# Memory keys and values of a two-block decoder kernel: the norm's root moves into the operand, values are made with tokens on rows, ScalarE copies them, and their blocks are dealt out over seven places

## What is computed

```python
def second_block(x, mem, mem_norm_gain, ...):
    mem_n = rms_norm_2(mem, mem_norm_gain)
    for layer in range(DEPTH):            # DEPTH = 2
        y = mlstm_mixer(...) if layer == 0 else stick_breaking_mixer(...)
        x = x + rms_norm_2(y, g[1])
        y = memory_cross_attention(rms_norm_2(x, g[2]), mem_n, xa_w_q, xa_w_kv, xa_w_o)
        x = x + rms_norm_2(y, g[3])
        y = swiglu_ffn(rms_norm_2(x, g[4]), ffn_w_gate_up, ffn_w_down)
        x = x + rms_norm_2(y, g[5])

def memory_cross_attention(h, mem_n, w_q, w_kv, w_o):      # XA_HEADS = 4, XA_HEAD_DIM = 256
    q = (h @ w_q).reshape(B, S, XA_HEADS, XA_HEAD_DIM)
    kv = (mem_n @ w_kv).reshape(B, 256, 2, XA_HEADS, XA_HEAD_DIM)
    k, v = kv[:, :, 0], kv[:, :, 1]
    s = einsum('bthd,bmhd->bhtm', q, k) * (XA_HEAD_DIM ** -0.5)
    o = einsum('bhtm,bmhd->bthd', softmax(s), v).reshape(B, S, D_MODEL)
    return o @ w_o
```

## Time and profile before

| | us |
|---|---|
| median of 3 runs (1766.02 to 1771.69) | 1766.06 |
| the profiled execution | 1770.89 |
| its span | 1769.1 |
| TensorE busy in it | 1690.5 (96%) |
| VectorE busy | 1186.5 (67%) |
| ScalarE busy | 936.5 (53%) |
| GpSimd busy | 332.4 (19%) |

### The profile page before, as it was taken

The page is one execution under the profiler, slowest core; times in us unless marked ns, Lnnn a source line. Parts: engine busy times, 40 slices in busy tenths (PEclk is TensorE's granted clock), DMA queues, the critical chain, the costliest instruction groups (busy, mean ns, idle before and its releaser), DMA issues.

```text
span 1769.1 us, 32699 instructions
## 1 busy us (share of the span) xinstructions
PE 1690.5 (96%) x13204; PEld 1615.9 (91%) x13204; DVE 1186.5 (67%) x2027; ACT 936.5 (53%) x1659; POOL 332.4 (19%) x304
## 2 busy tenths in 40 slices
PE   6999999999999989999999999999989999989997
PEld 6898889999997889999888999999979998889997
DVE  6999887555577745556577665866666667476665
ACT  5677765544455646544555444544455644454443
POOL 0100011243412112345111100000252110000025
PEclk8999999999999999999999999999999999989999
DMA  5433334555532245555334534455644343335663
GB/s 179 132 120 108 120 108 143 166 171 177 179 93 80 81 140 184 187 187 185 129 118 146 167 120 155 155 170 184 181 147 136 127 156 118 107 118 172 185 184 106
DMA packets 76325, 257.47 MB, mean 146 GB/s; under 512 B 8464, under 2 KB 12560, under 8 KB 75920
## 3 DMA queue, kind: packets, MB, share of 16 engines
q1 hardware_dynamic: 76176, 255.39, 45.1%
HBM read 254.31 MB, written 1.05 MB: 144 GB/s over the span
## 4 chain that ended last, share of the span: by engine, by line
PE 77%; DVE 12%; ACT 6%; issue 4%; POOL 1%; DMA 0%; POOLq 0%; DVEq 0%; SPq 0%; ACTq 0%
PE pb L140 75%; DVE WL L159 2%; DVE TMP L171 2%; DVE SCR L171 2%; ACT SCR L149 1%; ACT L156 1%; DVE SCR L159 1%; PE pb L143 1%; ACT WH L149 1%; DVE HNL L171 1%; POOL SCR L159 1%; ACT TMP L149 1%; ACT ASH L149 1%; DVE ASL L171 0%; ACT Rbuf L149 0%
## 5 line engine op out<-in xcount | busy, mean ns | idle before, releaser
L140 PE MATMUL pb<-HNH,WH 128*128 128x256 f32 (+1 forms) x2120 | 613.9, 290 | 6.1 <-DVE WL L159 1.9
L159 DVE TENSOR_TENSOR WL<-RAW,WH 128x1024 fp32r<-128x1024 f32 (+4 forms) x514 | 604.9, 1177 | 10.4 <-ACT WH L149 10.0
L140 PE MATMUL pb<-HNH,WL 128*128 128x256 f32 (+1 forms) x2120 | 603.1, 284 | 0.0
L140 PE MATMUL pb<-HNL,WH 128*128 128x256 f32 (+1 forms) x2120 | 602.8, 284 | 0.0
L149 ACT ACTIVATE WH<-RAW 128x1024 fp32r<-128x1024 f32 (+4 forms) x514 | 507.2, 989 | 154.7 <-PE pb L140 147.1
L140 PE MATMUL pb<-ASH,WH 128*128 128x256 f32 (+1 forms) x1688 | 493.4, 292 | 11.1 <-DVE WL L159 7.1
L140 PE MATMUL pb<-ASH,WL 128*128 128x256 f32 (+1 forms) x1688 | 483.2, 286 | 0.0
L140 PE MATMUL pb<-ASL,WH 128*128 128x256 f32 (+1 forms) x1688 | 482.9, 286 | 0.0
L140 PEld LDWEIGHTS pb<-HNH,WH 128*128 128x128 f32 x2120 | 402.1, 190 | 14.3 <-issue 6.8
L140 PEld LDWEIGHTS pb<-HNH,WL 128*128 128x128 f32 x2120 | 402.4, 190 | 0.0
L140 PEld LDWEIGHTS pb<-HNL,WH 128*128 128x128 f32 x2120 | 400.6, 189 | 1.0
(11 more groups left out here) (149 smaller groups left out, 1454.3 us busy)
## 6 DMA issues: line engine op xcount, KB each, us to landing
RAW<-in_w_gu SPq DMA_DIRECT2D x88, 512.0 KB, 3.8
RAW<-in_w_up SPq DMA_DIRECT2D x64, 512.0 KB, 3.5
RAW<-in_w_down SPq DMA_DIRECT2D x64, 512.0 KB, 3.5
RAW<-in_w_ssd SPq DMA_DIRECT2D x48, 512.0 KB, 3.5
RAW<-in_w_xkv SPq DMA_DIRECT2D x32, 512.0 KB, 3.5
RAW<-in_w_mlin SPq DMA_DIRECT2D x24, 512.0 KB, 3.5
RAW<-in_w_fd SPq DMA_DIRECT2D x32, 384.0 KB, 3.0
RAW<-in_w_sbqkv SPq DMA_DIRECT2D x24, 512.0 KB, 4.1
```

The costliest lines, as they stand in the source:

```text
L140: return self.eng.matmul(o, l, r, start=start, stop=stop, skip_group_check=skip) if self.eng else Nothing()
L159: return self.eng.tensor_tensor(o, a, b, op) if self.eng else Nothing()
```

## The change

- The memory chunks are multiplied by gain and root in place, once, by VectorE in steps 8 to 15 of `mlin` (`dve_mem_root`); the high and low parts are made from that without a scale. `RM` is not used when blocks leave PSUM any more.
- Values are made with tokens on the partitions: the memory's high and low chunks (128 tokens each) are the loaded operand, and the split weights are streamed, 256 columns (one head) at a time. A head's values take two blocks of weights as a pair, in two banks; both banks have to be free before the pair starts, and both are filled when it ends. The weights are laid out for this on the host.
- ScalarE copies keys and values out of PSUM (`act_fill`), where it waits for TensorE's end of the block or pair. VectorE only splits weights there. The transposes and the copies after them are gone.
- The fills are dealt out anew (in blocks): 5 in the last steps of mLSTM, 7 in the norm after `mlo`, 4 in the last steps of cross-attention 0, 5 in the norm after `xo0`, 5 in the norm after `fd0`, 2 in the last steps of the stick-breaking attention, 4 in the norm after `sbo`. In a norm one fill or none stands ahead of every second step m, and one fill (of two blocks) instead of two stands ahead of `pe_rest` after `sbo`.
- For the fills after `fd0` the memory's parts are made a third time (`mem2`), in `ASH[:, 0:8]`, during the eight last blocks of `fd0`.
- Cross-attention waits for the keys' copies at its first scores and for a head's value copies at that head's output product.

```diff
-    p += xkv[0][0:7] + out("mlo", xkv[0][7:16])
-    p += [("xq0", 0, m) for m in range(8)] + xkv[1][0:2] + out("xo0", xkv[1][2:8])
-    p += ffn(0)
-    p += [("sbqkv", 0, m) for m in range(24)] + xkv[1][8:12] + out("sbo", xkv[1][12:16])
+    p += xkv[0][0:5] + out("mlo", xkv[0][5:12])
+    p += [("xq0", 0, m) for m in range(8)] + xkv[0][12:16] + out("xo0", xkv[1][0:5])
+    p += ffn(0) + xkv[1][5:10]
+    p += [("sbqkv", 0, m) for m in range(24)] + xkv[1][10:12] + out("sbo", xkv[1][12:16])
...
-                q.wait_ge(*(eva if PLAN[i - 3][0] in ("up0", "up1", "wk") else evd)[i - 3])
+                q.wait_ge(*(eva if PLAN[i - 3][0] in ("up0", "up1", "wk", "xkv0", "xkv1") else evd)[i - 3])
...
-        FILL = {"mlo": [(0, "k", 7)] + [(0, "v", c) for c in range(8)],
-                "xo0": [(1, "k", m) for m in range(2, 8)], "sbo": [(1, "v", c) for c in range(4, 8)],
-                "xo1": [], "fd0": [], "fd1": []}
+        FILL = {"mlo": [("k", 0, 5), ("k", 0, 6), ("k", 0, 7), ("v", 0, 0), ("v", 0, 1)],
+                "xo0": [("k", 1, m) for m in range(5)],
+                "fd0": [("k", 1, 5), ("k", 1, 6), ("k", 1, 7), ("v", 1, 0)],
+                "sbo": [("v", 1, 2), ("v", 1, 3)], "xo1": [], "fd1": []}
+        FIRSTS = {"mlo": 2, "xo0": 2, "fd0": 2, "sbo": 1, "xo1": 0, "fd1": 0}
+
+        def fills_at(post, m):
+
+            rest = FILL[post][FIRSTS[post]:]
+            return rest[m // 2:m // 2 + 1] if m % 2 == 0 else []
...
+        def mem_parts(l, kind, m):
+            if l == 0:
+                return as_chunks("mem0", 8, 8, T2)
+            if kind == "k" and m < 5:
+                return as_chunks("mem0", 8, 8, T2)
+            if kind == "k" or m == 0:
+                return as_chunks("mem2", 0, 8, T2)
+            return as_chunks("mem1", 8, 8, T2)
+
+        def v_blocks(q, l, h):
+            return [q.block(f"xkv{l}", 0, 8 + 2 * h + j) for j in range(2)]
+
+        def pe_fill(q, kind, l, m):
+            xs = mem_parts(l, kind, m)
             if kind == "k":
+                pe_block(q, f"xkv{l}", 0, m, T2, xs)
+                return
+            ids = v_blocks(q, l, m)
+            for i in ids:
+                pe_bank_free(q, i)
+            for j in range(2):
+                q.wait_ge(*lo[ids[j]])
+                for t in range(2):
+                    o = bank_of(ids[t])[:, 0:256]
+                    for k in range(4):
+                        xh, xl, ready = xs[4 * j + k]
+                        wh = WH[:, ids[j] % NWS, 256 * k:256 * k + 256]
+                        wl = WL[:, ids[j] % NWS, 256 * k:256 * k + 256]
+                        q.wait_ge(*ready)
+                        q.matmul(o, xh[:, 128 * t:128 * t + 128], wh, j == 0 and k == 0, False)
+                        q.matmul(o, xl[:, 128 * t:128 * t + 128], wh, False, False)
+                        mm = q.matmul(o, xh[:, 128 * t:128 * t + 128], wl, False, j == 1 and k == 3)
+                mm.then_inc(*use(ids[j]))
+
+        def act_fill(q, kind, l, m):
+            if kind == "k":
+                i, b = act_block(q, f"xkv{l}", 0, m, T2)
+                q.wait_ge(*use[i])
                 if l:
                     q.wait_ge(*xs_[0, 3])
+                q.activation(KM[:, m, :], b, ACT.Copy).then_inc(*eva(i))
+                return
+            ids = v_blocks(q, l, m)
+            act_split(q, ids[1])
+            q.wait_ge(*use[ids[1]])
+            if l:
+                q.wait_ge(*xov[0, m])
+            for t in range(2):
+                q.activation(VM[:, t, 256 * m:256 * m + 256], bank_of(ids[t])[:, 0:256], ACT.Copy).then_inc(*eva(ids[t]))
+
+        def dve_fill(q, kind, l, m):
+            if kind == "k":
+                dve_block(q, f"xkv{l}", 0, m, T2)
             else:
+                dve_split(q, v_blocks(q, l, m)[1])
...
-            for f in fill[:2]:
+            for f in fill[:FIRSTS[post]]:
...
-                if m + 2 < len(fill):
-                    pe_fill(q, *fill[m + 2])
+                for f in fills_at(post, m):
+                    pe_fill(q, *f)
...
-        def act_mem(q, l, c):
-            q.wait_ge(s_mem, 16)
-            act_part(q, mem_tag(l), c, ASH[:, 8 + c, 0:T2], MR[:, c, :],
-                     use[AT["down1", 3, 7] if l == 0 else AT["fd0_5", 1, 7]], scale=cc("memn", c, 1))
-
-        def dve_mem(q, l, c):
-            q.wait_ge(*ah[mem_tag(l), c])
-            q.stt(ASL[:, 8 + c, 0:T2], MR[:, c, :], cc("memn", c, 1), ASH[:, 8 + c, 0:T2].bitcast(F32), ALU.mult,
-                  ALU.subtract).then_inc(*al(mem_tag(l), c))
+        def dve_mem_root(q, c):
+            q.wait_ge(*rms["mem"])
+            q.stt(MR[:, c, :], MR[:, c, :], cc("memn", c, 1), RM[:, :], ALU.mult, ALU.mult).then_inc(*memsc(c))
+
+        MEMPARTS = {"mem0": (8, lambda: use[AT["down1", 3, 7]]), "mem1": (8, lambda: use[AT["fd0_5", 1, 7]]),
+                    "mem2": (0, lambda: use[AT["fd0_5", 0, 7]])}
+
+        def act_mem(q, tag, c):
+            c0, free = MEMPARTS[tag]
+            act_part(q, tag, c, ASH[:, c0 + c, 0:T2], MR[:, c, :], free(), memsc[c])
+
+        def dve_mem(q, tag, c):
+            c0 = MEMPARTS[tag][0]
+            dve_part(q, tag, c, ASL[:, c0 + c, 0:T2], MR[:, c, :], ASH[:, c0 + c, 0:T2])
...
+        ML_FILL = [0, 1, 2, 4, 5]
...
-            return [(1, "k", n - 9)] if l == 0 and n > 8 else []
+            return [("v", 0, n - 6)] if l == 0 and n in (8, 9) else []
...
-                    q.wait_ge(*evd[AT[f"xkv{l}", 0, 7]])
-                    q.wait_ge(*xvc[l, 7])
+                    q.wait_ge(*eva[AT[f"xkv{l}", 0, 7]])
...
+                q.wait_ge(*eva[AT[f"xkv{l}", 0, 9 + 2 * h]])
...
                         act_block(q, fd_name(l, q4), q4 % 2, m, T2)
+                        if l == 0 and q4 == 3:
+                            act_mem(q, "mem2", m)
                         if q4 == 3:
                             act_square(q, post, m, Y[:, m, :], T2, yadd[l, 3, m])
...
                         i, b = dve_block(q, fd_name(l, q4), q4 % 2, m, T2)
+                        if l == 0 and q4 == 3:
+                            dve_mem(q, "mem2", m)
                         q.wait_ge(*use[i])
...
-                pe_fill(q, 1, "v", n - 24)
+                if n == 24:
+                    pe_fill(q, "v", 1, 1)
...
-        arr[f"xkv{l}"] = lay(f["xa_w_kv_2"][l], 1, 8)
+        kv = f["xa_w_kv_2"][l]
+        vv = kv[:, 1024:2048].reshape(2, 4, 128, 4, 256).transpose(3, 0, 2, 1, 4).reshape(1, 8, 128, 1024)
+        arr[f"xkv{l}"] = np.concatenate([lay(kv[:, 0:1024], 1, 8), vv], 1)
```

## The result

| | before | after |
|---|---|---|
| median of 10 runs each (before 1765.07 to 1773.45, after 1773.53 to 1781.91) | 1767.66 | 1777.43 |
| ratio, 95% interval | | 1.0046, 1.0030 to 1.0062 |
| profiled execution, its span | 1770.89, 1769.1 | 1781.91, 1780.1 |

The change makes the kernel slower by 0.46% in the ratio (8.1 us; the means are 1768.8 and 1776.9); the medians differ by 9.8 us, and the spans of the two profiled executions by 11.0. The forecast was 1776.

A forecast was written before the change was run, and what follows sets the result against it. TensorE, busy 96% of the span, was taken as the bound, so time could come only from its waits and small work. The terms summed to +9.7 us on a median of 1766.06, about 1776; range 1762 to 1787.

The forecast's parts named there:

- Point 3: Last eight `fd0` blocks: making `mem2` closes a ring of waits through four engines, 3.55 us a turn; +9.5 us.
- Rival A: The `mem2` loop in `fd0` doesn't bite, as TensorE has slack; about 1766 us, chance 0.15.
- Point 2: Norm after `fd0`: five fills, 14.3 us of blocks, lengthen it by only 7.5 us; -6.8 us.
- Point 1: Value blocks: 16 pairs of transposes go, most on a full TensorE; -3.4 us.
- Point 4: `sb` tail: two blocks instead of four leave waits of 3.4, 0.6 and 1.2 us; +5.0 us.
- Point 5: `ml` tail: two blocks fewer cost 5.7 us, an earlier root gives back 1.9; +3.8 us.
- Point 6: `mlo`, cross attention, `xo0`, `sbo`: bank wait +0.5, copies +0.8, VectorE's relief in the norms -1.2 and -1.8 us.
- Point 7: `mlin`: eight root multiplications of 0.47 us on VectorE, mostly in idle time; +0.3 us, bounds 0 and +2.
- Point 8: Both tails and before part 7: low clock after new waits, taken in two places; +3 us, bounds 0 and +6.
- Rival C: Slower through the clock: `fd0` loop, key blocks behind it, starts of `mlo` and `sbo` at 1.2 GHz; 1786, chance 0.16.
- Rival B: Norm chains: evictions and copies leaving VectorE shorten waits; 1759 us, or 1755 with tails half hidden; chance 0.09.
- D: Key/value product: new form costs more, 5% on 16 blocks +2.3 us, or a like gain; inside the forecast's 0.60.

The follow-up runs named there:

- The form alone: Changed kernel with all fills where they stood before the change and no third set of memory parts; 1764.26 us, ratio 0.9972.
- four parts: Changed kernel with `mem2` step behind eviction, `sb` tail value pair two steps later, seven `ml` tail key blocks, root multiplied by GpSimd; 1761.34 us, ratio 0.9957.
- the old places: Changed kernel with the fills where they stood before the change and the multiplication by the root on GpSimd; 1762.25 us, ratio 0.9961.

## Why the prediction was right, and where it was off

The time, 1777.43, is 1.4 above the forecast of 1776.0 and inside its range. That it is so near is in part luck: ten runs of the kernel before gave a median 1.6 above the three that the forecast started from, and the difference, +9.7 forecast and 9.8 measured by the medians (8.1 by the ratio), is a sum of stages that missed by up to 2.7 us with both signs. The interval excludes no change, but 0.46% lies just short of the line of 0.5% that the forecast drew between slower and same. By its own steps:

- **Point 3, the ring: right, in size too.** Forecast +9.5. Undoing it brought 9.0 in the medians, 8.3 by the ratios and 9.6 us between the traces. TensorE's share of it is 7.4 us of waits and 2.3 of low clock in the two blocks behind (8.0 us instead of 5.7). That low clock is no cost on top: part 7 was ready at 1316.95, and in the run with seven key blocks in the `ml` tail, where the low stretch was shorter, TensorE waited 0.58 us for it at 1317.01 and the two blocks still took 8.1. The turn was forecast at 3.55 and measured at 3.51; with the wide splits 3.9 was forecast and 4.1 measured, since GpSimd's sum takes 1.63 beside a 1024-wide split. Only the waiter was another: not the key block for part 7 but the sum of squares in front of it, for GpSimd's sum of a pair of squares, which hangs on the same ring. Rival A (the loop doesn't bite) is out. The Trainium skill ("SBUF — State Buffer", section "SBUF: two separate sides") let me ask whether VectorE's part would itself be held up by the shared port. The trace says no, 0.43 us: GpSimd is idle in that moment of the ring. Only the first part, at 1290.08, met one of GpSimd's sums (1289.17 to 1290.42), and it took 0.62.
- **Point 2, five fills behind `fd0`: -6.8 forecast, -5.6 measured** without the ring, 0.9 us of new waits included. The chain from the logarithm to the last operand half was forecast at 16 us and is (1321.80 to 1337.6).
- **Point 1, transposes: supported.** The form alone gained 4.7 (1.9 to 8.1), and they are gone from the fills; -3.4 is inside.
- **Point 4, `sb` tail: right.** The wait is 3.43 for the 3.4 forecast; with 1.75 us of low clock the stage took +5.7, for 4.2 plus 1.5. The two waits that were to follow, 0.6 and 1.2, are not there (0.20 is): the slow sums ran through them. With the clock kept up they are 0.42 and 0.41, and the low clock then costs 0.9 us, not 1.75.
- **Point 5, `ml` tail: right in the sum, wrong in its make-up.** `mlo` resumed at 968.4, 2.1 us earlier than forecast, against an earlier `mlin` by 0.9; without its 1.55 us of low clock the stage is +2.5, not 3.8. The waits are 1.15 and 2.70.
- **Point 6: the small terms were right (+0.9 for +0.8, 0.52 us for the bank forecast at 0.5), the gains in the norms came smaller.** After `xo0` TensorE's idle time fell by 0.4 us (2.22 to 1.86) for the -1.2 forecast. After `sbo` VectorE has 2.3 us less to do (17.29 busy for 19.56), and TensorE's waits fell from 2.29, 0.59 and 0.98 to 1.54, 0.40 and 0.32, which is the sign that step 6 named. But part of the last one is slow sums: in the run with seven key blocks in the `ml` tail, where the clock stayed at 1.00 there, the waits are 1.54, 0.40 and 0.99, and the stage is about 1.2 us shorter without the transposes, for 1.8 forecast. In the changed kernel's profile the low clock took 1.4 of that back.
- **Point 7, roots: `mlin` took +1.8 instead of +0.3,** inside its bounds of 0 and +2, near the upper. I had put eight operations "mostly in idle time" because VectorE had idle time in sum. With four parts, moving them to GpSimd brought the stretch from 72.1 or 72.7 us to 70.6, where it was 70.4 before; at the old places it took only 0.2 off, so that the roots are the whole cause is not shown. Idle in sum doesn't say that the operations ahead of a waited-for one are free.
- **Point 8, clock: right in kind, wrong in number of places.** Forecast +3 in two places, bounds 0 and +6. TensorE lost 2.3 us of work to the low clock behind the ring, 1.55 in `mlo`, 1.75 in the `sb` tail and 1.4 after `sbo` (the last sums and the first `xa1` block take 5.3 us, from 1490.68 to 1495.95, instead of 3.9), 7.0 in four places. Not all of it lengthens the kernel: about none behind the ring and 0.9 in the tail, by the points above, so some 4 us are on the path. This is an estimate from those rows. What offset it in the profiled difference is 2.7 and 0.8 us in code that the change doesn't touch, and 1.3 in the `ml` tail.
- **Rival C came half true.** The ring itself kept the upper level, 2.4 GHz: 1.00 from 1290 to 1305, over waits of 0.97 and 1.49. The clock fell to the lower level, 1.2 GHz, behind the wait of 3.95, behind those of 2.70 and 3.43 at the tails and after `sbo`, and came back within a block or two. The Trainium skill ("TensorE: Matmul & The Clock Gate", section "HAM oscillation — how this bites in real kernels") tells of short bursts that start at the low clock one after another, with waits of about 3 to 5 us between them. The ring's waits were shorter, and the trace shows no low clock there; the forecast took the page's case for nearer than it was. After `sbo` (waits of 1.54, 0.40 and 0.32) the clock was 0.50 from 1488.0 to 1494.8.
- **Rival B (VectorE's relief speeds the norms up)** is out: the wait after `sbo` stayed over 1 us. **D (the new form costs more)** is out as well: the form alone is faster, and the 48 matmuls of a value pair start 0.120 us apart (1007.56 to 1013.31), against 0.119 in the kernel before.

## What to carry to other kernels

When a new operation is put into an engine's fixed order, draw the loop that its wait closes with what the other engines already wait for, and add up one turn; if the turn is longer than TensorE's step, the place in the order costs more than the operation. Here two lines further down were worth 8 to 9 us, and the whole redistribution of blocks, once mended, was worth nothing that can be measured against the old places. Blocks moved into a gap must leave another place, and a place that looks full (17.00 of 17) can have a wait right behind it: here it was 3.43 us.

## What was not expected of the hardware

- Past the gate, TensorE went on at half speed (matmuls 0.21 us apart instead of 0.12) behind every wait of 2.7 to 4.6 us in these profiles and lost up to 2.3 us of work. Behind shorter waits the same code did so in some executions and not in others: behind 1.54 and 0.40 us after `sbo`, and behind waits of 2.62 and 2.51 us that all kernels have ahead of the gate. Products that nobody reads keep the level: twelve sums went from 3.65 us to 2 x 1.14, and with 19 such products in the wait of 4.58 us after `xo1` the stretch went from 14.2 us to 12.6.
- An fp32 product of 128x128 constants counts as two instructions and takes 0.23 us, as long as two of the fp32r ones with 256 columns.
- Code that is the same up to the gate reached it between 861.6 and 871.2 us in the profiles of these kernels, and the runs of one kernel spread over 3 to 12 us, with mean granted clocks from 0.975 to 0.991 over all runs. In most kernels the shorter times go with the higher clocks. The arrivals at the gate show it: the two earliest, 861.6 and 862.8, are the only profiles that kept the upper level behind both of those waits (0.99 on average up to the gate, against 0.98 at 868.5 and 871.2). So terms of 1 to 3 us can be read from stretches of a trace, hardly from medians.
